# A decoder trunk on one core: tiles 0 and 1 of nine softmax groups transposed and multiplied together

## The reference, cut to what matters

```python
# MoBA heads, and the NSA heads' selected and window branches: causal masked softmax
s = einsum('bhqd,bhkd->bhqk', q, k) * scale
p = softmax(where(mask, s, NEG)) * mask
o = einsum('bhqk,bhkd->bhqd', p, v)
# NSA: o = gate0 * o_compressed + gate1 * o_selected + gate2 * o_window
# stick-breaking heads
a = exp(log_sigmoid(z) - tail)            # tail: reversed cumulative sum of softplus(z)
o = einsum('bhqk,bhkd->bhqd', a, v)
```

## Time and profile before

| | before |
|---|---|
| median of 3 runs | 1683.88 us |
| the profiled execution's own time | 1683.82 us |
| its span | 1682.1 us |
| PE busy | 1672.4 us, 99% |
| weight loads (PEld) busy | 1368.7 us, 81% |
| DVE / ACT / POOL busy | 655.2 / 726.4 / 841.7 us |

### The profile page before, as it was taken

How to read it: one execution, slowest core, us unless ns; L and a number is a source line. 1 busy time by engine, 2 the same in 40 slices (tenths; PEclk the granted TensorE clock), 3 DMA queues, 4 the chain that set the end, 5 groups by cost and what they waited for, 6 DMA issues and landing times.

```text
span 1682.1 us, 23253 instructions
## 1 busy us (share of the span) xinstructions
PE 1672.4 (99%) x9217; PEld 1368.7 (81%) x9217; DVE 655.2 (39%) x1423; ACT 726.4 (43%) x1386; POOL 841.7 (50%) x553
## 2 busy tenths in 40 slices
PE   9999999999999999999999999999999999999998
PEld 7888776888898888888888887768888988888886
DVE  3454665163272222311233456652442622232113
ACT  6325777363361222232362357764543522222322
POOL 4447668464443444445623567665634344444552
PEclk9999999999999999999999999999999999999999
DMA  6234111242122223232323340112413223332322
GB/s 227 76 97 135 51 26 52 77 150 75 64 98 95 88 96 100 76 125 100 111 92 100 94 138 26 26 51 88 163 51 105 84 75 101 100 100 76 105 96 75
DMA packets 101191, 154.15 MB, mean 92 GB/s; under 512 B 4396, under 2 KB 76380, under 8 KB 101084
## 3 DMA queue, kind: packets, MB, share of 16 engines
q1 hardware_dynamic: 98572, 147.16, 26.7%
q10 hardware_dynamic: 2512, 5.51, 1.0%
HBM read 150.56 MB, written 2.10 MB: 91 GB/s over the span
## 4 chain that ended last, share of the span: by engine, by line
PE 97%; ACT 1%; POOL 1%; issue 1%; DVE 0%; DVEq 0%; ACTq 0%; POOLq 0%
PE banks L1730 27%; PE banks L1732 27%; PE banks L1731 27%; PE banks L2045 4%; PE banks L2098 4%; PE banks L2074 4%; PE banks L1858 1%; PE banks L1774 1%; PE banks L2094 0%; PE banks L2242 0%; PE banks L1762 0%; POOL w_lo L795 0%; ACT w_hi L937 0%; ACT rows L906 0%; PE banks L1972 0%
## 5 line engine op out<-in xcount | busy, mean ns | idle before, releaser
L795 POOL TENSOR_TENSOR w_lo<-raw,w_hi 128x1024 fp32r<-128x1024 f32 (+2 forms) x262 | 629.1, 2421 | 656.3 <-ACT w_hi L937 643.6
L937 ACT ACTIVATE w_hi<-raw 128x1024 fp32r<-128x1024 f32 (+2 forms) x264 | 259.8, 1027 | 643.8 <-PE banks L1732 635.4
L1730 PE MATMUL banks<-w_hi,a_lo 128*128 128x512 f32 (+1 forms) x864 | 332.5, 385 | 0.1
L1732 PE MATMUL banks<-w_hi,a_hi 128*128 128x512 f32 (+1 forms) x864 | 330.1, 382 | 0.0
L1731 PE MATMUL banks<-w_lo,a_hi 128*128 128x512 f32 (+1 forms) x864 | 330.0, 382 | 0.0
L1730 PE MATMUL banks<-a_hi,w_lo 128*128 128x512 f32 x768 | 299.6, 390 | 0.0
L1732 PE MATMUL banks<-a_hi,w_hi 128*128 128x512 f32 x768 | 298.8, 389 | 0.0
L1731 PE MATMUL banks<-a_lo,w_hi 128*128 128x512 f32 x768 | 298.8, 389 | 0.0
L1730 PEld LDWEIGHTS banks<-w_hi,a_lo 128*128 128x128 f32 x864 | 162.4, 188 | 32.6 <-issue 1.7
L1732 PEld LDWEIGHTS banks<-w_hi,a_hi 128*128 128x128 f32 x864 | 162.2, 188 | 31.5
L1731 PEld LDWEIGHTS banks<-w_lo,a_hi 128*128 128x128 f32 x864 | 162.3, 188 | 30.4
(11 more groups left out here) (278 smaller groups left out, 2441.5 us busy)
## 6 DMA issues: line engine op xcount, KB each, us to landing
raw<-in_ffn_w_up SPq DMA_DIRECT2D x44, 1024.0 KB, 5.0
raw<-in_ffn_w_down SPq DMA_DIRECT2D x20, 1024.0 KB, 4.9
raw<-in_w_in SPq DMA_DIRECT2D x19, 1024.0 KB, 5.0
raw<-in_x_wk SPq DMA_DIRECT2D x8, 1024.0 KB, 5.2
raw<-in_x_wv SPq DMA_DIRECT2D x8, 1024.0 KB, 4.9
raw<-in_x_wq SPq DMA_DIRECT2D x8, 1024.0 KB, 5.1
raw<-in_x_wo SPq DMA_DIRECT2D x8, 1024.0 KB, 4.9
raw<-in_cmp_wk SPq DMA_DIRECT2D x4, 1024.0 KB, 5.5
```

The lines of the kernel that those rows point to most:

```text
L795: inc(pool.tensor_tensor(lo_half(u, half), raw_half(u, half), hi_half(u, half).bitcast(F32), ALU.subtract), lo_made, n)
L937: inc(act.activation(hi_half(u, half), raw_half(u, half), ACT.Copy), hi_made)
L1730: pe.matmul(dst, st_lo, mv_hi, start=first, stop=False)
L1732: return pe.matmul(dst, st_hi, mv_hi, start=False, stop=last)
```

## The change

For the tile-1 items of nine softmax groups (all but the first group, whose tile 1 is item 1) the function `behind` is true: items 5, 13, 17, 22, 26, 35, 39, 44 and 48. Their transposes come 3 steps behind their scores instead of 4, and their values 4 instead of 5, so both fall into the steps of tile 0 of the same group. Tile 1's transposes go to columns 128 to 383 of banks 4 and 5, beside tile 0's in columns 0 to 127, and so don't wait for the copies of tile 0. The copies of tile 0 wait for the transposes of both tiles. All else stays. The diff, in full but for its context:

```diff
+def behind(i):
+    return 4 <= i < NI and SOFT[i] and ITEMS[i][1] == 1
+
+TURN_STEP = [i + LAG_T - behind(i) for i in range(NI)]
+VALUE_STEP = [i + LAG_V - behind(i) for i in range(NI)]
...
 # ACT, copy_T(i)
-act.wait_ge(pT_psum.sem, pT_psum.at(l, psums(i, KIND[i] == "sb")))
+act.wait_ge(pT_psum.sem, pT_psum.at(l, psums(i + behind(i + 1), KIND[i] == "sb")))
...
-inc(act.activation(pT(i)[:, 0], bank(4, n), ACT.Copy), copied_act)
+inc(act.activation(pT(i)[:, 0], bank(4, n, P * behind(i)), ACT.Copy), copied_act)
...
-if 0 <= i - LAG_T < NI:
-    copy_T(i - LAG_T)
+for j in range(NI):
+    if TURN_STEP[j] == i:
+        copy_T(j)
...
 # DVE, copy_T(i)
-dve.wait_ge(pT_psum.sem, pT_psum.at(l, psums(i, 1)))
+dve.wait_ge(pT_psum.sem, pT_psum.at(l, psums(i + behind(i + 1), 1)))
 wait_pT(dve, l, i)
-inc(dve.tensor_copy(pT(i)[:, 1], bank(5, item_keys(i))), copied_dve)
+inc(dve.tensor_copy(pT(i)[:, 1], bank(5, item_keys(i), P * behind(i))), copied_dve)
...
 # PE, transposes(i)
-if i >= 1:
+if i >= 1 and not behind(i):
     pe.wait_ge(copied_act.sem, copied_act.at(l, i))
...
-if hp and soft_before(i):
+if hp and soft_before(i) and not behind(i):
     pe.wait_ge(copied_dve.sem, copied_dve.at(l, soft_before(i)))
 for k in range(ITEMS[i][1] + 1):
-    ins = pe.transpose(bank(4 + hp, P, P * k), probs(i, hp)[:, P * k:P * k + P], ident[:])
+    ins = pe.transpose(bank(4 + hp, P, P * k + P * behind(i)), probs(i, hp)[:, P * k:P * k + P], ident[:])
...
-if LAG_T <= i < NI + LAG_T:
-    transposes(i - LAG_T)
-if i >= LAG_V:
-    values(i - LAG_V)
+for j in range(NI):
+    if TURN_STEP[j] == i:
+        transposes(j)
+for j in range(NI):
+    if VALUE_STEP[j] == i:
+        values(j)
```

More of the change, by code:

```diff
@@ L1583, in _ @@
                             block_copy(j)
-                    if i >= LAG_T:
-                        copy_T(i - LAG_T)
+                    for j in range(NI):
+                        if TURN_STEP[j] == i:
+                            copy_T(j)
                     if 1 <= i < NI + 1 and KIND[i - 1] != "cmp":
```

## The result

The changed kernel takes 1697.45 us, the median of 6 runs (1695.94 to 1697.71), beside 1683.80 us for the kernel before (6 runs, 1683.65 to 1683.92). The ratio is 1.008 with a 95% interval of 1.007 to 1.009: slower, by 13.65 us. I had forecast 1695.4, in a range of 1689.5 to 1701. The profiled execution took 1695.94 us (span 1694.2), 12.12 us more than the profiled one of before, and is the shortest of the six. The other five lie 1.3 to 1.8 us above it; why is a finding of its own, further down.

A forecast was written before the change was run, and what follows sets the result against it. PE, busy 99% of the span, was taken as the bound. Per layer 3.3 + 1.4 - 0.3 + 1.4 = 5.8 us, +11.6 in two layers, on 1683.8 gave 1695.4 us; range 1689.5 to 1701.

The forecast's parts named there:

- Block changes, 0.15 us each, 5.4 us in all: Attention loops: joining each pair's transposes and values saves PE two changes of block kind, 0.30 us a pair, 18 pairs.
- the removed waits for copies cost nothing today: PE's transposes in the attention loop: dropping their waits for copies gains 0, since PE doesn't idle.
- Rival (5): Joined blocks save nothing, the next item's weight load draining PE all the same: +17.0 us, 1700.8; chance 8%.
- The new wait at E + 0.76: ACT's exponentials, behind tile 1's copy, start 0.76 us after E, the old end of the previous group's last values.
- New heads +3.3 a layer: Items 12, 21, 34 and 43, opening heads without fill work: values wait for the late copy of oT, +3.3 us together.
- Windows +1.4: Window groups at items 16, 38 and 47: scores or output projection wait for late exponentials, +1.4 us a layer.
- VectorE: nothing: VectorE's copy has the same new wait, but only a reciprocal and scalings used three steps on stand behind: no cost.
- Item 26 -0.3: Pair of items 25 and 26: 0.9 us of fill work covers the wait, so it keeps its gain, -0.30 us a layer.
- Item 4, +1.43: Item 4's stick-breaking exponentials and a cast of weights delay the copy of oT: values 1.59 late, net +1.43 us a layer.
- Layer 1 like layer 0: Layer 1's attention loop was taken to repeat layer 0's 5.8 us, giving +11.6 us for both.
- Rivals (1) to (3): Only switches count, 1678.4, 5%; only new-head places cost, windows gain, 1690.9, 12%; stalls a third, cancelling the gain, 1684, 5%.
- Rival (4): ACT doesn't catch up and delays next-step copies, 0.4 us at 16 places: +6.4 more, 1701.8; chance 10%.

The follow-up runs named there:

- e3: Changed kernel with only item 26 of each layer joined to its tile 0: 1683.43 us, -0.44 against the kernel before.
- e1: Changed kernel with a third probT buffer, so tile 1's copy no longer waits for the previous group's values: 1681.96 us, before 1683.87, ratio 0.9989.
- e2: Changed kernel, two buffers, with ACT's copy of tile 1 back in its old place behind the exponentials and the copy of oT: 1682.34 us, ratio 0.9991.
- e4: Changed kernel with only items 13, 22, 35 and 44 joined (new heads): 1690.54 us, +6.67 against the kernel before.
- e7: Changed kernel with only items 17, 39 and 48 joined (window groups): 1686.37 us, +2.59 against the kernel before.
- e5: Changed kernel with only item 5 of each layer joined: 1688.62 us, six runs from 1687.20 to 1690.38, +4.84 against the kernel before.
- e6: Changed kernel with three probT buffers and ACT's copies of items 5, 13, 22, 35 and 44 in their old place: 1680.60 us, before 1683.78, ratio 0.9981.
- e10: Changed kernel with all joined but item 5: 1692.90 us (5 runs, 1692.78 to 1693.01).

## Why the prediction was right, and where it was off

- **Block changes, 0.15 us each, 5.4 us in all: right for the joined blocks, short for the kernel.** The joined blocks have the lengths worked out, 0.80 and 0.80; by 0.16 a block (0.37 + 0.59 - 0.80) they make 5.8. Stalls of 18.2 us less 12.1 measured leave 6.1 us saved, and 7.8 if stalls are counted from start to start. What lies over 5.8 is mostly the small waits that PE's busy time hid (1.3) and the cheaper change to the memory's keys (0.17 or so, as in e3, at two places of a layer). So the reason given for "the removed waits for copies cost nothing today", that PE doesn't idle, isn't enough: a wait can hide in PE's busy time, as the 0.17 us at item 48 did. Rival (5), that joined blocks save nothing, falls: e1, with 4.9 us of stalls left in two layers, would be at 1688.8; it is at 1682.0. By the rule that PE pulls a weight load ahead of matmuls in flight (the Trainium skill, TensorE: Matmul & The Clock Gate, Step-by-step) joining would earn nothing either; these blocks don't bear that out.
- **The new wait at E + 0.76: right, 0.07 short.** In the changed kernel the values of item 11 would have ended 0.44 sooner, at 205.64, without the pair's longer transposes, and ACT's exponentials start at 206.47, which is 0.83 later. From there to the copy of oT 0.69, from its start to PE 0.75: 2.27 for 2.21. e1 and e2 show that this wait at this place is the cause: without it, or with it behind the exponentials, the 15 us are gone.
- **New heads +3.3 a layer: right** (e4: +3.34). **Windows +1.4: right** (e7: +1.30). The output projection starts 2.42 behind E (295.26; E is 292.84, the end of item 46's values at 293.28 less the 0.44 of the longer transposes), foreseen 2.33. A third of PE's idle time there, 0.33 of 0.96, is put down to VectorE's copy, which the prediction had called free:

```profile
293.39 0.38 ACT L1124 ACTIVATE probT<-banks 128x256 f32<-128x256 f32 x1 [1.03 <-PE banks L2109]
293.40 0.42 DVE L1580 COPY probT<-banks 128x256 f32<-128x256 f32 x1 [0.35 <-PE banks L2109]
```

But ACT's copy of the same item ends at 293.77, 0.05 before VectorE's, and the projection waits for ACT's exponentials until 295.26 in any case, so "VectorE: nothing" holds. **Item 26 -0.3: -0.22,** for a copy of ACT that PE now meets too early.
- **Item 4, +1.43: the stall was right (values at 180.43, forecast 180.34), a second one at item 8 was missed.** The prediction took each pair's saving as kept, and never asked whether PE, come sooner, finds the next copy of oT done. At item 8 it doesn't. ACT and PE in the kernel before, then ACT in the changed one:

```profile
192.42 0.60 ACT L1079 ACTIVATE oT<-banks 128x512 f32<-128x512 f32 x1
193.17 0.44 PE L2098 MATMUL banks<-probT,proj 128*64 128x128 f32 x4
...
189.53 1.06 ACT L1094 ACTIVATE proj<-proj 128x1024 f32<-128x1024 f32 x1 [1.37 <-DVE proj L1551]
```

The values of item 8 started 0.15 behind the end of that copy already, the hand-over time, so there was nothing to spare, and what joining items 4 and 5 saves is waited for here. ACT isn't late from the stall, as e5's expectation had it: it stands idle 1.37 us for VectorE in between. And e1, e2 and e6, whose stall at item 4 is down to 0.58, 0.31 and 0.31 us, have the wait at item 8 too (0.29, 0.39, 0.42), while e10, without item 5 joined, has none. It costs 0.6 us in two layers. The lowest run of e5 is +1.71 a layer for +1.43 + 0.28. The stall at the piece of the memory's keys (0.28) is of the same kind.
- **The clock was left out altogether.** No term and no rival gave PE a cost for having been idle, beyond the idle time. One fall of 1.5 us in most runs is the larger part of the error. In numbers: +11.6 foreseen, +0.6 for item 8, +1.45 for the fall make 13.65, and 13.65 were measured. The agreement to the last digit is luck; e3, e4, e7 and the lowest run of e5 sum to +12.2, and the lower-level runs of the change are at +12.1 and +12.3.
- **Layer 1 like layer 0: right,** stall by stall.
- Rivals (1) to (3) fall with the stalls that were foreseen, all of them seen: 1.19 us at the four new heads (1.0 to 1.2 foreseen), 1.73 at item 4 (1.7), 0.54 twice in the windows (0.7), 0.96 in two pieces at the end (over 1). Rival (4) falls because the two stalls that weren't foreseen are 0.28 us each, not 0.4 at 16 places, and neither comes from ACT staying late.

What stays open: which executions fall to 1.2 GHz behind the stall and which don't. Of 11 runs of the change 8 lie about one fall above the others, none two, while two of e5's six, by their times, fell in both layers. The idle time before it is the same 1.73 us in the profiles with and without a fall, so nothing in these records tells them apart.

## What to carry to other kernels

When a step is moved earlier, look at what stands behind it in each in-order queue, not only at whether its own wait is met in time: the same wait cost 15 us ahead of the exponentials (some 1.5 of them the fall of the clock) and nothing behind them. Look too at what comes just in time today: here two copies of oT ended 0.14 and 0.15 us before the values that need them, and time saved on PE ahead of such a place is waited for again. A gain from fewer, larger blocks is real where the trace shows a fixed cost per block, but it is small change (0.3 us a pair here) beside one stall of an engine that is 99% busy, so give the copy a spare buffer before moving it. And where a stall can't be avoided, put work that is ready in front of the wait: that paid twice here, for the time itself and for the clock.

## What was not expected of the hardware

An idle time of 1.73 us on PE, ended by value products and with matmuls and transposes at full clock before it, was followed in some executions by 3.4 us at 1.2 GHz (granted clock 0.50), at a cost of about 1.5 us each; in others, of the same program and with the same idle time, by none. Stalls of 1.19 us, up to eight in a run, were followed by none in the ten runs of e4 and e10. Times that lie on levels some 1.5 us apart, in a kernel whose runs otherwise agree to 0.3 us, were the first sign, and the granted clock by stretches the proof.
